# Even attention: each group's values as a 64-column product, its probability sums added on VectorE

## The reference, cut to what matters

```
s = jnp.einsum('bqkgd,bskd->bkgqs', q, k, preferred_element_type=jnp.float32) * (HEAD_DIM ** -0.5)
p = jax.nn.softmax(s, axis=-1).astype(v.dtype)
return jnp.einsum('bkgqs,bskd->bqkgd', p, v)
```

## Time and profile before

| | us |
|---|---|
| median of 3 runs (3037.8 to 3041.22) | 3039.82 |
| the profiled execution, its own time | 3045.2 |
| its span | 3043.5 |
| even attention, first scores to last logits (402 to 972) | 570 |

### The profile page before, as it was taken

The page is one execution under the profiler, slowest core; times in us unless marked ns, Lnnn a source line. Parts: engine busy times, 40 slices in busy tenths (PEclk is TensorE's granted clock), DMA queues, the critical chain, the costliest instruction groups (busy, mean ns, idle before and its releaser), DMA issues. The chain is left out here.

```text
span 3043.5 us, 31441 instructions
## 1 busy us (share of the span) xinstructions
PE 2390.5 (79%) x10535; PEld 1759.1 (58%) x10536; DVE 1548.6 (51%) x2093; ACT 985.5 (32%) x1305; POOL 617.3 (20%) x601
## 2 busy tenths in 40 slices
PE   5499877689895459999992776995997837999980
PEld 0278744456563038888882664773665725888770
DVE  2255453244332145665553546984773235566754
ACT  1122133224231034554442211112652105456540
POOL 0133345411111210000001224220312331000002
PEclk9999978899997569999996887997998967999995
DMA  9211077635312967776645553335862345687936
GB/s 386 93 42 42 28 224 247 221 79 121 98 39 92 320 225 267 259 262 250 227 173 161 198 168 123 100 111 153 209 157 81 115 167 203 226 311 275 355 135 235
DMA packets 323974, 546.08 MB, mean 179 GB/s; under 512 B 123785, under 2 KB 168341, under 8 KB 317718
## 3 DMA queue, kind: packets, MB, share of 16 engines
q1 hardware_dynamic: 209298, 396.46, 38.4%
q0 software_dynamic: 26096, 85.62, 8.2%
q10 hardware_dynamic: 88468, 62.58, 6.7%
HBM read 432.75 MB, written 126.51 MB: 184 GB/s over the span
## 5 line engine op out<-in xcount | busy, mean ns | idle before, releaser
L2741 DVE TENSOR_TENSOR ex_gu_lo<-mw_gu,ex_gu_hi 128x2048 fp32r<-128x2048 f32 x128 | 287.4, 2288 | 78.8 <-ACT ex_gu_hi L2661 78.5
L2661 ACT ACTIVATE ex_gu_hi<-mw_gu 128x2048 fp32r<-128x2048 f32 x128 | 237.5, 1910 | 166.7 <-DVE ex_y L2788 160.2
L1771 PE MATMUL at_ps_o<-at_pT,at_v_one 128*128 128x512 f32 x336 | 181.8, 623 | 13.6 <-ACT at_total L1546 13.4
L2636 POOL TENSOR_TENSOR ex_at<-ex_slots,ex_nil 128x1 int32<-128x1 int32 x53 | 16.6, 313 | 805.8 <-PE ex_ps_x L2813 800.5
L2819 PE MATMUL ex_ps_g<-ex_gu_hi,ex_xT_hi 128*128 128x512 f32 x408 | 170.0, 417 | 8.3 <-issue 5.2
L2819 PE MATMUL ex_ps_y<-ex_d_hi,ex_hT_hi 128*128 128x512 f32 x408 | 166.7, 409 | 9.1 <-DVE ex_d_lo L2741 7.7
L1534 ACT ACTIVATE at_pT<-at_ps_s 128x512 f32<-128x512 f32 x168 | 99.6, 594 | 221.8 <-PE at_ps_s L1764 210.4
L2741 DVE TENSOR_TENSOR ex_d_lo<-mw_d,ex_d_hi 128x2048 fp32r<-128x2048 f32 x64 | 143.8, 2288 | 54.1 <-ACT ex_d_hi L2661 54.1
L2819 PE MATMUL ex_ps_g<-ex_gu_lo,ex_xT_hi 128*128 128x512 f32 x408 | 164.8, 404 | 0.0
L2819 PE MATMUL ex_ps_g<-ex_gu_hi,ex_xT_lo 128*128 128x512 f32 x408 | 164.8, 404 | 0.0
L2819 PE MATMUL ex_ps_y<-ex_d_lo,ex_hT_hi 128*128 128x512 f32 x408 | 161.9, 397 | 0.0
(11 more groups left out here) (469 smaller groups left out, 5747.5 us busy)
## 6 DMA issues: line engine op xcount, KB each, us to landing
mw_gu<-in_moe_w_gate SPq DMA_DIRECT2D x32, 2048.0 KB, 10.7
mw_gu<-in_moe_w_up SPq DMA_DIRECT2D x32, 2048.0 KB, 15.7
mw_d<-in_moe_w_down SPq DMA_DIRECT2D x32, 2048.0 KB
y_d<-ex_y ACTq DMA_DIRECT2D x51, 512.0 KB
mod_mod_w<-in_ada_w SPq DMA_DIRECT2D x24, 1024.0 KB, 11.0
ro_mod_w<-in_ada_w SPq DMA_DIRECT2D x24, 1024.0 KB, 34.8
y_d<-at_zero POOLq DMA_DIRECT2D x36, 512.0 KB, 6.2
edge_d<-rows_d ACTq DMA_DIRECT2D x64, 160.0 KB, 2.7
```

What stands on the lines that cost most here:

```text
L1771: nc.tensor.matmul(ps_o[:, :], v_one[:, kt, g:g + 2, :].rearrange("p a d -> p (a d)"), pT[u % 3][:, :], start=(u == plan.first[i, g]), sto ...
L2636: nc.gpsimd.tensor_tensor(at[:, :], slots[:, bass.ds(within(n, most), 1)], nil[:, :], ALU.add).then_inc(S["at_ready"], 1)
L2661: nc.scalar.activation(dst, src, ACT.Copy).then_inc(sem, 1)
L2741: sub = lambda dst, a, b, sem: nc.vector.tensor_tensor(dst, a, as_f32(b), ALU.subtract).then_inc(sem, 1)
```

## The change

The value product of a step uses only the group's 64 value columns, straight from `k.v0`, and writes its own half of `ps_o`: partitions 0 to 63 for group 0, 64 to 127 for group 1. Steps of the two groups alternate, `(i, 0, kt), (i, 1, kt)`, and events come in pairs of steps: the side work of both positions, two scores, two values. One drain for each tile copies the whole bank. The probability sums are built on VectorE: for each group an accumulator `part` takes `pT` of the first key tile as a copy and adds the others. A new event 'sums' at position 0 of the next tile multiplies both accumulators by 64 columns of ones into the two halves of a `ps_t` bank, and ScalarE copies it to `sums`. `pT` has four buffers, and ScalarE's exponential of step u waits for values and addition of step u - 4. `v_one` and its preparation are gone.

```diff
-            for g in range(2):
-                self.first[i, g] = len(self.steps)
-                self.steps += [(i, g, kt) for kt in self.key_tiles(i)]
-                self.last[i, g] = len(self.steps) - 1
+            start = len(self.steps)
+            self.steps += [(i, g, kt) for kt in self.key_tiles(i) for g in range(2)]
...
-            for u in range(a, b):
-                for what in [x for at, x in side if self.step_of(at, x, b - a) == u - a]:
+            for u in range(a, b, 2):
+                for what in [x for at, x in side if u <= a + self.step_of(at, x, b - a) <= u + 1]:
                     self.event(*what)
-                if u + 2 < len(self.steps):
-                    self.event('scores', u + 2)
-                self.event('values', u)
-                if u in (self.last[i, 0], self.last[i, 1]):
-                    self.event('drain', i, self.steps[u][1])
+                for s in (u + 2, u + 3):
+                    if s < len(self.steps):
+                        self.event('scores', s)
+                for s in (u, u + 1):
+                    self.event('values', s)
+            self.event('drain', i)
...
+        return [(0, ('sums', i)),
...
-        if what in ('q', 'max', 'shift', 'mixed', 'h'):
+        if what in ('q', 'max', 'shift', 'sums', 'mixed', 'h'):
...
-        v_one = ph.sb("v_one", [P, NT, 3, HD])
+        ones = ph.sb("ones", [P, HD])
+        part = [[ph.sb(f"part{p}{g}", [P, 512]) for g in range(2)] for p in range(2)]
...
-        pT = [ph.sb(f"pT{i}", [P, 512]) for i in range(3)]
+        pT = [ph.sb(f"pT{i}", [P, 512]) for i in range(4)]
...
-                        if u >= 3:
-                            act.wait_ge(S["valued"], u - 2)
-                        nc.scalar.activation(pT[u % 3][:, :], ps_s[u % 3][:, :], ACT.Exp).then_inc(S["exp_done"], 1)
+                        if u >= 4:
+                            act.wait_ge(S["valued"], u - 3)
+                            act.wait_ge(S["added"], u - 3)
+                        nc.scalar.activation(pT[u % 4][:, :], ps_s[u % 3][:, :], ACT.Exp).then_inc(S["exp_done"], 1)
...
-                        nc.scalar.activation(sums[own, :], ps_o[other, :], ACT.Copy)
-                        nc.scalar.activation(total[own, :], ps_o[own, :], ACT.Copy).then_inc(S["drained"], 1)
+                        nc.scalar.activation(total[:, :], ps_o[:, :], ACT.Copy).then_inc(S["drained"], 1)
+                    elif what == 'sums':
+                        ps, read = filled(act, *ev)
+                        if i:
+                            act.wait_ge(S["aT_ready"], i)
+                        nc.scalar.activation(sums[:, :], ps[:, :, :].rearrange("p c t -> p (c t)"), ACT.Copy).then_inc(read, 1)
...
+                    if what == 'values':
+                        u, (i, g, kt) = i, steps[i]
+                        acc = part[i % 2][g]
+                        dve.wait_ge(S["exp_done"], u + 1)
+                        if u == plan.first[i, g]:
+                            if i >= 2:
+                                filled(dve, 'sums', i - 2)
+                            nc.vector.tensor_copy(acc[:, :], pT[u % 4][:, :]).then_inc(S["added"], 1)
+                        else:
+                            dve.wait_ge(S["added"], u - 1)
+                            nc.vector.tensor_tensor(acc[:, :], acc[:, :], pT[u % 4][:, :], ALU.add).then_inc(S["added"], 1)
...
-                        pe.wait_ge(S["exp_done"], u + 1)
-                        if u == plan.first[i, g] and (i or g):
-                            pe.wait_ge(S["drained"], plan.drains[(i, 0) if g else (i - 1, 1)] + 1)
-                        nc.tensor.matmul(ps_o[:, :], v_one[:, kt, g:g + 2, :].rearrange("p a d -> p (a d)"), pT[u % 3][:, :],
-                                         start=(u == plan.first[i, g]), stop=(u == plan.last[i, g])).then_inc(S["valued"], 1)
+                        if g == 0:
+                            pe.wait_ge(S["exp_done"], u + 2)
+                        if u == plan.first[i, 0] and i:
+                            pe.wait_ge(S["drained"], i)
+                        own = slice(g * HD, (g + 1) * HD)
+                        nc.tensor.matmul(ps_o[own, :], k.v0[:, kt, own], pT[u % 4][:, :], start=(u == plan.first[i, g]),
+                                         stop=(u == plan.last[i, g]), skip_group_check=True).then_inc(S["valued"], 1)
+                    elif what == 'sums':
+                        pe.wait_ge(S["added"], plan.last[i, 1] + 1)
+                        ps, full = bank(*ev)
+                        for g in range(2):
+                            mm = nc.tensor.matmul(ps[g * HD:(g + 1) * HD, :, :].rearrange("p c t -> p (c t)"), ones[:, :], part[i % 2][g][:, :],
+                                                  start=True, stop=True, skip_group_check=True)
+                        mm.then_inc(full, 1)
```

More of the change, by code:

```diff
@@ L1256, in __init__ @@
         for i, tile in enumerate(self.tiles):
+            start = len(self.steps)
+            self.steps += [(i, g, kt) for kt in self.key_tiles(i) for g in range(2)]
             for g in range(2):
-                self.first[i, g] = len(self.steps)
-                self.steps += [(i, g, kt) for kt in self.key_tiles(i)]
-                self.last[i, g] = len(self.steps) - 1
-        self.events, self.banks, self.drains = [], {}, {}
+                self.first[i, g], self.last[i, g] = start + g, len(self.steps) - 2 + g
+        self.events, self.banks = [], {}
         self.next_bank, self.uses = 0, [0, 0, 0]
@@ L1303, in finish @@
     def finish(self, i):
[L1304 removed]
+        return [(0, ('sums', i)),
+                (1, ('invert', i, 0)), (1, ('invert', i, 1)), (2, ('invert', i, 2)), (3, ('invert', i, 3)), (3, ('normal', i)),
                 (4, ('mixed', i)), (6, ('out', i, 0)), (9, ('out', i, 1)), (12, ('square', i)), (13, ('mean', i)),
@@ L1323, in event @@
             self.next_bank = (b + 1) % 3
-        if what == 'drain':
-            self.drains[a] = len(self.drains)
         self.events.append((what, *a))
@@ L1539, in _ @@
                     elif what == 'drain':
-                        g = ev[2]
-                        act.wait_ge(S["valued"], plan.last[i, g] + 1)
+                        act.wait_ge(S["valued"], plan.last[i, 1] + 1)
                         if i:
                             act.wait_ge(S["aT_ready"], i)
-                        own, other = slice(g * HD, (g + 1) * HD), slice((1 - g) * HD, (2 - g) * HD)
-                        nc.scalar.activation(sums[own, :], ps_o[other, :], ACT.Copy)
-                        nc.scalar.activation(total[own, :], ps_o[own, :], ACT.Copy).then_inc(S["drained"], 1)
+                        nc.scalar.activation(total[:, :], ps_o[:, :], ACT.Copy).then_inc(S["drained"], 1)
[4 more added lines that the diff above has]
+                        nc.scalar.activation(sums[:, :], ps[:, :, :].rearrange("p c t -> p (c t)"), ACT.Copy).then_inc(read, 1)
                     elif what == 'q':
@@ L1581, in _ @@
                 nc.gpsimd.memset(nmx[:, :], 0.0).then_inc(S["nmx_zero"], 1)
-                nc.gpsimd.memset(v_one[:, :, 1, :], 1.0).then_inc(S["ones_ready"], 1)
+                nc.gpsimd.memset(ones[:, :], 1.0).then_inc(S["ones_ready"], 1)
                 nc.gpsimd.memset(zero[:, :], 0.0).then_inc(S["zero_ready"], 1)
@@ L1638, in _ @@
                         split_w(i - 2, i - 1)
-                    if what == 'q':
+                    if what == 'values':
[9 more added lines that the diff above has]
+                            nc.vector.tensor_tensor(acc[:, :], acc[:, :], pT[u % 4][:, :], ALU.add).then_inc(S["added"], 1)
+                    elif what == 'q':
                         g = ev[2]
@@ L1664, in _ @@
                         c = slice(ev[2] * P, (ev[2] + 1) * P)
-                        dve.wait_ge(S["drained"], 2 * i + 2)
+                        emptied(dve, 'sums', i)
                         nc.vector.reciprocal(sums[:, c], sums[:, c]).then_inc(S["summed"], 1)
```

8 lines of the change are left out of this document (3 added, 5 removed).

## The result

The changed kernel took 3054.61 us (median of 9 runs, 3045.24 to 3060.12), the kernel before 3039.82 (median of 9 on the same chip, 3032.92 to 3043.18). The ratio is 1.0041, 95% interval 1.003 to 1.0053: slower by 0.4%, 12 us. The prediction was 3050 and slower.

A forecast was written before the change was run, and what follows sets the result against it. TensorE bounds full latent tiles, dependent chains the context tiles, transfers tile 2; with the change VectorE's in-order work delays 'out'. Tile terms, clock falls included, sum to +10 us on 3039.8: 3050, own range 3040 to 3062, overall range 3018 to 3072.

The forecast's parts named there:

- The change of the array's shape: TensorE, around each pair of value products: switching costs 0.15 us a pair, +12.6 us over 84 pairs, bounds 0 and 25.
- TensorE's own sum: TensorE, even attention: overlap -71.6, shape switches +12.6, 'sums' +10, drain waits -13.4, together -62 us.
- VectorE's total: VectorE, even attention: 168 new additions or copies at 0.61 us, +102 us, 12.2 for a latent tile.
- The walk through a full tile: Full latent tile in list order: +3.0 to 'out', then -1.4, -2.1, -0.4; together -0.9, giving 50.8 us.
- the +3.0 ahead of 'out': Tile start to 'out' in a full tile: 16.0 us instead of 13.0, because of VectorE's additions.
- The fall ahead of 'out': Thin TensorE stretch from 8.1 to 14 us: lower clock adds 1.8 us to the next pair, 1.0 to 'out'.
- The second fall: After TensorE's wait before 'h': with half a chance the clock falls, costing 2.4 us, counted as +1.2 a full tile.
- The sum by tile: Even attention: tiles 4, 5, 8 +9.3, tile 6 +0.5, tile 9 -1.5, context tiles +0.5 each, tile 0 +1; +10 us.
- Rival 1: Even attention: VectorE is late but the clock stays up, -0.9 a full tile, about -6, 3034 us; chance 0.25.
- Rival 2: Latent tiles: TensorE stays the bound, 'out' no later than 13 us, -35 to -40, 3002 us; chance 0.15.
- Rival 3: Tiles: additions meet GpSimd's work, delaying `aT` and 'norm'; both clock falls in every tile, +3 each, 3070 us; chance 0.12.
- Rival 4: Value pairs: the two products don't overlap, 1.71 us plus the switch, +25 more, 3075 us; chance 0.06.

The follow-up runs named there:

- kernel 6: Changed kernel with a scores product between the two value products of each pair, so they no longer run side by side: 3091.03 us, ratio 1.0151 to before.
- kernel 5: Changed kernel plus throw-away TensorE products ahead of two maxima products in the third pair of tiles 1, 4, 5 and 8: 3044.19 us, ratio 1.0 to before.
- Kernel 1: Kernel before with events, side work included, in pairs of steps and four pT buffers; values 128 wide, no additions: 3055.94 us, ratio 1.0045 to before.
- kernel 2: Kernel before with only scores and values in pairs, side work spread over the two positions: 3045.15 us, ratio 1.0003 to before.
- Kernel 3: Changed kernel with side work spread over the two positions of a pair, value products still side by side: 3052.88 us, ratio 1.0027 to before.
- kernel 10: Changed kernel with side work spread, 'out' products cut in three and most of the next tile's maxima placed between the parts: 3038.15 us, ratio 0.9977 to before.
- kernel 9: Kernel before with the next latent tile's maxima moved from positions 1 to 15 to positions 6 to 16: 3042.05 us, ratio 0.9981 to before.

## Why the prediction was right, point by point

**TensorE's products.** The overlap is right: a pair's four passes show as 1.08 us, and kernel 6 shows that it is real. The change of the array's shape is mis-sized. A pair of steps without side work, in tile 9 of the changed kernel:

```profile
926.33 1.08 PE L1787 MATMUL at_ps_o<-at_pT,v 128*64 128x512 f32 x4
927.33 0.50 PE L1777 MATMUL at_ps_s<-at_q_both,k_both 128*128 128x512 f32 x1
927.68 0.40 PE L1778 MATMUL at_ps_s<-at_q_rest,at_k_one 65*128 65x512 f32 x1
...
928.15 0.40 PE L1778 MATMUL at_ps_s<-at_q_rest,at_k_one 65*128 65x512 f32 x1
928.48 1.08 PE L1787 MATMUL at_ps_o<-at_pT,v 128*64 128x512 f32 x4
```

A pair of steps takes 2.15 us. Four passes at 0.43 and four scores products at 0.23 are 1.79, so the round trip costs 0.36: 0.10 ahead of the passes (they start 0.33 after the last scores product, not 0.23) and 0.26 behind them (the second product starts 1.35 us after the first pass, not 1.09). The prediction took 0.15 with an upper bound of 25 us; 84 times 0.36 is 30 us. The 0.37 that it read in the earlier trace rows was nearer than the half of it that it took, and TensorE's own sum becomes some -45 us in place of -62. Against two steps of 1.33 a pair saves 0.51 us, 43 us over 84, where 59 was taken. The Trainium skill's page "TensorEngine Tiling (Array Packing)", Key Properties, says that changing the tiling mode drains TensorE. The trace agrees in that both changes of the shape cost time.

**VectorE's total.** 102 us were taken; the additions took 127.0 and the copies 10.2 on the changed kernel's profile. In tile 8 the sum came close (13.0 us more, 12.2 taken), but with a part in it that was not summed: two pairs of additions collide with GpSimd, 2.35 and 2.46 us in place of 1.28. In tile 1 GpSimd is busy 36.87 us, and an addition's median is 1.10 us, not 0.68. The collisions that the prediction left out of its sum, at most 1.5 us a tile, were 2.2 us of VectorE's time in each of tiles 4, 5 and 8.

**The walk through a full tile.** Right, and nearly so in its parts. Without the clock it gave 50.8 us, 0.9 less than before; kernel 5, where the clock stays up, took 50.7 to 50.9. For the changed kernel, tile 5, counted from the last value product: 'out' at 18.05 us (16.0 and 1.8 for the clock), 'out' to step 10 17.4 (16.3 and 1.0), then 10.05 to `h` (10.4), 8.1 to the end (8.2). Some of that is luck: the low part of 'mixed' ended at 13.6 (13.9) because `aT` was ready 0.6 us earlier than walked and the additions behind it took 1.1 us longer. Behind 'out' the change of the array's shape costs 0.2 us more a pair than walked, while TensorE stands 1.5 us before `h` and not 3.

**The cause given for the +3.0 ahead of 'out'** ("the additions cause it"). Only half right, and this is the step that failed. The walk had the bunched order in it and so the right time, but it gave the whole delay to the additions. Kernel 1 has 'out' 3.3 us later and a ratio of 1.0045 without one addition; kernel 2, with the side work spread, has 0.8 and 1.0003. Kernel 3 shows the other half: with the side work spread and the additions in place 'out' is still at 16.9. Either one is enough. So a reader who undid only one of them would still have a late 'out'; the side work alone was tried (kernel 3), the additions alone were not. The walk should have been made with and without each of them.

**The clock.** The fall ahead of 'out' came in all of tiles 1, 4, 5 and 8, and its size was about right: 2.8 us in tile 5 and 1.6 in tiles 4 and 8 (against kernel 5), 2.8 taken. The second fall, ahead of `h`, had half a chance and 1.2 us: it did not come in tiles 4, 5 and 8, where TensorE waits 1.5 us there. It came in tile 6, where two additions beside GpSimd's shift took 3.43 us and TensorE waited 3.08.

**The sum by tile.** Tiles 4, 5 and 8: +3.5 us together where +9.3 was taken: the second fall (half of 2.4 a tile, 3.6 in all) did not come, and the first cost 1.6 in place of 2.8 in two of them. Tile 6: +3.7 where +0.5 was taken, since both falls came. Tiles 1 to 3: -0.7 where +0.5 was taken: as forecast, tile 2's transfers evened out tile 1's +7.9, and tile 3 became 4.6 longer. Tile 9: -1.9 (-1.5), tile 7 +1.0 (+0.5), tile 0 -1.1 (+1). Even attention as a whole ended 4.5 us later where +10 was taken. So 3050 came near the median of 3054.61 partly by errors of both signs, and because the median stands 5.7 us above the profiled execution. What makes the executions of one kernel differ by 10 us is open; the stretch from the last copy into `total` to the end, nearly all of it the same code in all kernels here, took from 2106 to 2117 us in their profiled executions.

**The rivals.** Rival 1 (the clock stays up, 3034) did not happen; kernel 5, which makes it happen in four tiles, has a ratio of 1.0, some 3040. Rival 2 (TensorE stays the bound, 'out' no later than 13 us into the tile) is what kernel 10 makes: 47.1 us a tile. But it is worth far less than its 35 to 40 us: the first four tiles give back 8.7 us, and the sum was too high. Behind tile 2 there are five latent tiles and not seven (tiles 4, 5, 6, 8 and 9), which at 6.2 us each is 31. Rival 3's collision came in every latent tile from tile 1 on, in tiles 4, 5 and 8 both ahead of 'out' and at the shift, but the second fall of the clock that it wanted came in tile 6 and not in those three. Rival 4 is kernel 6, ratio 1.0151: 3086 in place of 3075.

## What to carry to other kernels

A change that takes work from the bounding engine and gives it to one with half its time idle is worth nothing as long as that engine's idle time lies elsewhere: count both loads from one dependency to the next, not by the tile. And set the reordered kernel beside the old one with its own best order: here the two came out level (kernels 10 and 9). When two steps are joined so that their products can run side by side, join only those; side work bunched with them meets its own banks, and that alone cost 0.4% here. Look, too, for gaps on TensorE behind which its clock falls: here two waits of 1.6 and 2.4 us cost another 1.6 to 2.8 us in products at the 1.2 GHz level, and products that computed nothing were cheaper than the gap.

## What the runs showed of the hardware

- Two float32 products of 64 columns into two halves of a bank, two passes each, show as 1.08 us, where one of 128 columns shows as 1.02. The round trip to and from products of full width costs 0.36 us by the starts (0.10 ahead, 0.26 behind).
- Fifteen products of 512 columns that computed nothing kept the granted clock at 1.00 through a stretch in which VectorE held TensorE up, and shortened the tile by 1.6 to 2.8 us.
- Two additions with both inputs in SBUF took 1.28 us on VectorE alone, 2.35 beside a GpSimd subtraction of 1.58, 3.07 beside a GpSimd addition of 2.36. The page "SBUF — State Buffer" of the Trainium skill (two separate sides) says that a VectorE operation with two SBUF inputs and a GpSimd operation that reads SBUF take their shared ports by an exclusive lock for a whole instruction. The trace agrees: the second addition ended 0.55 and 1.15 us after GpSimd's instruction.
